# GpSimd computes the low part of the two weight units for the dilated heads' keys in place of VectorE

## What is computed

```python
for l in range(DEPTH):
    h = rms_norm(x, g_mix[l])
    proj = h @ w_in[l]
    ...
    qa = (rms_norm(c_q, q_norm[l]) @ w_uq[l]).reshape(b, s, HEADS_A, QK_NOPE + QK_ROPE)
    kva = (rms_norm(c_kv, kv_norm[l]) @ w_ukv[l]).reshape(b, s, HEADS_A, QK_NOPE + V_DIM_A)
    ...
    o_a = dense_attention(qa, ka, kva[..., QK_NOPE:])
    pb = p_b.reshape(b, s, 3, HEADS_B, HEAD_DIM)
    o_b = dilated_sliding_attention(rope(pb[:, :, 0], pos), rope(pb[:, :, 1], pos), pb[:, :, 2])
    ...
    x = x + mixed @ w_out[l]
    h2 = rms_norm(x, g_mlp[l])
    x = x + jnp.square(jax.nn.relu(h2 @ w_mlp_in[l])) @ w_mlp_out[l]
return rms_norm(x, g_final)
```

## Time and profile before

| | |
|---|---|
| median of 3 runs | 2924.04 us (2922.69 to 2928.27) |
| the profiled execution's own time | 2928.63 us |
| its span | 2926.6 us |
| TensorE busy | 2850.3 us (97%) |
| VectorE busy | 1719.2 us (59%) |
| ScalarE busy | 1057.6 us (36%) |
| GpSimd busy | 141.4 us (5%) |

### The profile page before, as it was taken

One profiled execution on the slowest core, in us unless ns is written; L12 is line 12 of the kernel. 1 busy time (PEld: TensorE's weight loads), 2 busy tenths in 40 slices (PEclk: granted clock), 3 DMA queues, 4 the chain that ended last, 5 costly groups with the idle time before them and its releaser, 6 DMA issues.

```text
span 2926.6 us, 39906 instructions
## 1 busy us (share of the span) xinstructions
PE 2850.3 (97%) x14640; PEld 2437.3 (83%) x14640; DVE 1719.2 (59%) x2998; ACT 1057.6 (36%) x1976; POOL 141.4 (5%) x253
## 2 busy tenths in 40 slices
PE   7999999999999999999998999999999999999998
PEld 7998788878888888888798988888788888888886
DVE  5651787885555455455666337788755455455457
ACT  5332777873311111111243236777732111111113
POOL 0000331000000000000000011300000000000000
PEclk9999999999999999999999999999999999999999
DMA  5556875313111111111146577743221111111111
GB/s 196 176 191 159 199 187 122 87 44 117 42 47 54 43 46 54 43 46 62 45 177 199 163 189 192 180 101 87 73 72 44 43 57 43 43 57 43 43 62 70
DMA packets 182359, 285.34 MB, mean 97 GB/s; under 512 B 48848, under 2 KB 138576, under 8 KB 172496
## 3 DMA queue, kind: packets, MB, share of 16 engines
q1 hardware_dynamic: 171600, 254.16, 29.9%
q0 software_dynamic: 10624, 29.41, 3.6%
HBM read 210.60 MB, written 72.88 MB: 97 GB/s over the span
## 4 chain that ended last, share of the span: by engine, by line
PE 85%; DVE 5%; issue 3%; DMA 3%; ACT 2%; DVEq 1%; SPq 0%; ACTq 0%; POOLq 0%
PE ps L1445 24%; PE ps L1265 20%; PE ps L1460 18%; PE ps L1340 7%; PE ps L1354 6%; PE ps L1386 5%; PE ps L1396 2%; PE ps L1231 1%; PE ps L1304 1%; DMA biasC<-in_bias_c 1%; DMA values<-vst 1%; PE ps L1379 1%; DVE x L1184 1%; DVE hn L925 1%; DVE vbuf L1171 1%
## 5 line engine op out<-in xcount | busy, mean ns | idle before, releaser
L1460 PE MATMUL ps<-w_dn,hid 128*128 128x512 f32 x3072 | 713.9, 391 | 1.3
L1445 PE MATMUL ps<-hT,w_up 128*128 128x512 f32 x3072 | 702.5, 389 | 3.3 <-DVE hT L908 3.3
L1460 PEld LDWEIGHTS ps<-w_dn,hid 128*128 128x128 f32 x3072 | 573.5, 188 | 132.9 <-DVE x L1184 14.0
L1445 PEld LDWEIGHTS ps<-hT,w_up 128*128 128x128 f32 x3072 | 576.1, 188 | 123.2 <-ACT rbuf L858 3.7
L1265 PE MATMUL ps<-ws,hT 128*128 128x384 f32 (+3 forms) x3072 | 608.6, 356 | 6.5 <-DVE hT L908 5.3
L1265 PEld LDWEIGHTS ps<-ws,hT 128*128 128x128 f32 x3072 | 536.0, 190 | 52.1 <-DVE hT L908 5.8
L1184 DVE TENSOR_TENSOR x<-ps,x 128x512 f32<-128x512 f32 x512 | 343.0, 688 | 224.2 <-PE ps L1460 224.0
L1171 DVE TENSOR_TENSOR vbuf<-rbuf 128x512 f32<-128x512 f32 x128 | 88.5, 692 | 371.0 <-ACT rbuf L858 371.0
L808 ACT ACTIVATE pT<-ps 128x512 fp32r<-128x512 f32 (+1 forms) x448 | 240.5, 582 | 144.0 <-PE ps L1354 141.9
L908 DVE TENSOR_TENSOR pT<-ps,pT 128x512 fp32r<-128x512 f32 (+1 forms) x448 | 281.4, 663 | 8.2 <-ACT pT L808 7.2
L858 ACT ACTIVATE rbuf<-ps 128x512 f32<-128x512 f32 x128 | 76.6, 598 | 553.9 <-PE ps L1445 553.9
(11 more groups left out here) (85 smaller groups left out, 2175.4 us busy)
## 6 DMA issues: line engine op xcount, KB each, us to landing
raw<-in_wstream SPq DMA_DIRECT2D x76, 1024.0 KB, 4.8
head<-feats SPq DMA_DIRECT2D x192, 256.0 KB, 6.3
feats<-tst SPq DMA_DIRECT2D x128, 192.0 KB, 2.5
values<-vst POOLq DMA_DIRECT2D x32, 384.0 KB, 3.1
head<-values SPq DMA_DIRECT2D x24, 512.0 KB, 4.0
biasC<-in_bias_c SPq DMA_DIRECT2D x16, 768.0 KB, 11.5
raw<-in_wstream SPq DMA_DIRECT2D x12, 768.0 KB, 5.9
x_park<-x SPq DMA_DIRECT2D x16, 512.0 KB, 8.9
```

Source lines behind the costliest of these rows:

```text
L1445: last = pe.matmul(ps[:, k % 2, :], w_up[slot_of(l, 1 if first else 0)][:, w1, kt, ft * P:(ft + 1) * P], hT[:, w2, kt, sh * 512:(sh + 1) * ...
L1460: last = pe.matmul(ps[:, 2 + m % 4, :], hid[slot_of(l + 1, slot)][:, w1, ft, s * P:(s + 1) * P], w_dn[slot_of(l, 0 if last_group else 1)][ ...
```

## The change

GpSimd computes the low part of units 6 and 7 of each layer, between its stores of values: unit 6 behind the store of `uv 1`, unit 7 behind that of `uv 2`. VectorE leaves both out, in both layers. Since `split_lo` is a plain counter which two engines now raise, GpSimd waits for the unit before, and VectorE, ahead of the `bv` units, for both `bk` units.

```diff
+            def split_rest(l, job, half):
+
+                u = unit_of(job, half)
+                n = unit_len(job, half)
+                off = half * unit_len(job, 0)
+                pool.wait_ge(split_hi, l * NU + u + 1)
+                pool.wait_ge(split_lo, l * NU + u + 2)
+                hold(pool)
+                s = ws[slot_of(l, SLOT[job])]
+                pool.tensor_tensor(s[:, LO, off:off + n], raw[:, u % 2, 0:n], words(s[:, HI, off:off + n]),
+                                   ALU.subtract).then_inc(split_lo, 1)
+
             for l in range(DEPTH):
                 for vt, e in enumerate(VSTAGED):
...
                                    words(vst[:, k, 0:nh, :].rearrange("p h d -> p (h d)"))).then_inc(vst_out[k], 16)
+                    if e[1:] in (("uv", 1), ("uv", 2)):
+                        split_rest(l, "bk", e[2] - 1)
...
                 dve.wait_ge(split_hi, l * NU + u + 1)
+                if job == "bv":
+                    dve.wait_ge(split_lo, l * NU + unit_of("bk", 1) + 1 + 2)
...
                     if e[0] == "split":
-                        split_job(l, e[1], e[2])
+                        if e[1] != "bk":
+                            split_job(l, e[1], e[2])
```

## The result

| | before | after |
|---|---|---|
| median of 16 runs each | 2924.41 us (2921.26 to 2928.27) | 2930.36 us (2925.07 to 2938.82) |
| ratio | | 1.0021, interval 1.0015 to 1.0028 |
| the profiled execution's own time | 2928.63 us | 2928.79 us |
| its span | 2926.6 us | 2927.0 us |

The change costs 6.0 us, 0.21%, with an interval of 0.15% to 0.28%. It lies inside the range that was forecast and just beyond the 0.2% named there. In both kernels TensorE has the same work in it.

The account below looks back on a forecast made before the run. TensorE, busy 97% of the span, was taken as the bound, with its next work hanging on R. Terms 7.2 - 0.55 + 2.9 = +9.6 us gave 2933.6 us on the median (2938.2 us profiled); range 2927 to 2943 us.

Parts of the forecast that it names:

- R: Moment ScalarE may write `ur 2` into `tst`, after stores of `bq 7`; forecast 7.2 us later in layer one, 0.55 earlier in two.
- the wait of its 13th matmul: In `acc bk 0`, TensorE would wait 1.6 and 1.3 us for GpSimd's unit 7, 2.9 us in all.
- the subtraction: One unit's low part on GpSimd, two passes over the inputs: 3.5 us, between 1.76 and 5.3 us.
- GpSimd's start on `uv 2`: GpSimd would store `uv 2` at R + 2.93, for 0.54 us, and then subtract unit 7.
- the reload: Ahead of GpSimd's first subtraction, in the first layer, an instruction listed as ISA would cost 6.0 us.
- the slow subtraction: Rival, chance 0.17: GpSimd's subtraction takes three passes, 5.3 us, and the reload 7.1 us; +17.9 us, 2942 us.
- reload for nothing: Rival, chance 0.14: the reload ahead of GpSimd's first subtraction costs nothing; R 1.2 us later in layer one, not 7.2.
- The landing behind the load: From SP's start of the load of unit 8 to R: 6.0 us, ends 5.5 and 7.7.
- the 2.72 us wait: TensorE's wait for VectorE's low parts near unit 6 would go or shrink, worth 0 while the ScalarE stall covers it.
- the waits for ScalarE: TensorE's stalls behind the wait for VectorE, 2.33 and 5.57 us before, would be about 10 and 5 to 8 us.
- VectorE held up by GpSimd: Rival, chance 0.12: VectorE's last `ur 2` instructions stand until GpSimd's subtraction ends; about +1 us on the forecast, 2934.6 us.
- what sets R is SP's order: SP starts unit 8's load before the stores of `bq 7`; R comes 7.7 and 9.4 us after the load's start.

Follow-up runs that it names:

- Unit 6 alone: The changed kernel with only unit 6's subtraction on GpSimd and unit 7 kept on VectorE: 2926.78 us, ratio 1.0012 to the kernel before.
- the pair of kernels with late loads: Kernel before and changed kernel, each with SP's loads of units 8 and 9 behind the stores of `ur 2` and `ur 3`: 2925.10 and 2933.37 us.
- The extra subtraction: Kernel before, plus a 1024-column GpSimd subtraction behind the stores of `uv 1` and `uv 2`, its result unused: 2924.12 us, ratio 0.9997.
- the best kernel: Kernel before with the load of unit 8 behind the stores of `ur 2` and VectorE's unit 6 behind the low part of `uq 2`: 2916.14 us, ratio 0.9971.

## Why the prediction was right, and where it was wrong

**Right: the direction and the two places. The size was partly luck.** The forecast was +9.6 us and slower; measured were +6.0 us, and the loss lies at the two places that it named, the chain from unit 6 to R and `acc bk 0` with the wait of its 13th matmul. Its sizes for the subtraction (3.5 us, measured 3.43 to 3.45), for SP's step behind it (0.08 us, measured 0.09), for GpSimd's start on `uv 2` (R + 2.93, measured R + 2.93 and R + 2.92) and for unit 7 (R + 7.12, measured R + 6.96 and R + 6.95) held. The 3.5 us were the author's estimate, two times 1.76 us; 3.44 us are 1.95 times the 1.76 us of the earlier trace rows. The 0.15 us for GpSimd's start was an allowance that no row gave; 0.10 and 0.01 us are measured. That TensorE would want unit 7 at R + 5.55 and R + 5.79 is an estimate too: of the 24 matmuls' 5.36 and 5.60 us the second twelve get 2.22 us, half of the 4.45 us of the next 24, and the first twelve the rest. The largest term of the sum, though, was not there at all, and only because other terms came out larger does the time lie just beyond the 0.2% and not at the +3.5 us of the forecast's own sum without it.

**The step that failed: the reload at 6.0 us.** It was 6.0 of the 9.6 us. No run shows this term, nor the 7.1 us that the slow subtraction has in its place. The first subtraction of the program starts 0.10 us behind the store, with the two rows of 37 ns in front of it, and that of the second layer, which has no such rows, 0.01 us behind its own. So the instruction costs at most 0.1 us where it could delay anything; "reload for nothing", which makes R 1.2 us later in the first layer and not 7.2, was the true case. What the instruction does, and whether some of its work lies where GpSimd stood idle, no run here shows.

**The rest was mis-sized the other way.** Without the reload the forecast's own sum was 1.2 - 0.55 + 2.9 = +3.5 us; the stretch shows +5.4. The landing behind the load was good: 6.0 us assumed, 5.78 and 6.81 measured, and R moved by +0.85 and +0.06 where +1.2 and -0.55 were forecast without the reload. The second layer's `acc bk 0` went as forecast, with a slow first half and a wait of 1.26 us: 9.36 us from R to its end, where the forecast's terms make 9.31. The first layer's took 10.92 us where they make 9.38. The forecast had the first half slow there too, as before, and the second at 2.2 us. But TensorE's wait for ScalarE was short now (0.51 us), the transposes and the first twelve matmuls ran at a clock of 1.00 (0.60 and 2.33 us), and TensorE was at the 13th at R + 4.18 and waited 2.83 us in place of 1.6. That longer wait is no loss of its own, since unit 7 came when it was forecast. The loss is what followed: the second twelve took 3.91 us, at a mean clock of 0.56, in place of 2.2. That the clock can be low behind the wait was in no term of the sum.

**Wrong: the 2.72 us wait was to shrink, and the waits for ScalarE were to be about 10 and 5 to 8 us.** The first grew to 4.62 and 4.54 us, and the others fell to 0.51 and 1.90. (There are two such waits in each layer, not three as the prediction says.) The forecast was right that the wait for VectorE is worth 0 as long as ScalarE's stall covers it, and this cut both ways: the growth cost little or nothing either. Unit 6 alone shows the exchange (4.62 up, 0.24 left), and the pair of kernels with late loads shows the price of the whole change where the cover is gone, 8.3 us.

**The rival that came true beside it: VectorE held up by GpSimd.** It was given 0.12 and +1 us. The hold is there at all four subtractions, 3.73 to 3.82 us each, and it is why VectorE's busy time rose: 4 x (3.76 - 0.25) = +14.0, less 4 x 1.76 = 7.0, makes +7.0 of the 7.8 us. VectorE's addition is recorded 0.16 to 0.27 us ahead of GpSimd's subtraction each time, and is held all the same. The price was right in kind: the stores of `bq 7` started 1.00 us behind the load (119.64 to 120.64) where 0.35 were assumed. The extra subtraction shows that a shorter hold, covered, costs nothing that can be measured; but no run here had the delay of the units without a hold, so what each has of the 6.0 us stays open.

**Right in the main: R hangs on SP's order.** With the load moved behind the stores, R comes some 3 us earlier in each layer; the forecast's "what sets R is SP's order" was too strong, since 3.30 and 4.90 us of waiting for the stores remain. What this place had to give was in the order, of SP's load and of the subtraction among VectorE's own instructions, not in VectorE's busy time.

## What to carry to other kernels

Before work is moved off an engine because others wait for it, ask what they wait for next: here the wait for VectorE stood in front of a longer chain (a buffer behind stores, the stores behind a load), and changing the order of one load and one subtraction gave 8.2 us where moving the subtraction to an idle engine lost 6.0. An idle GpSimd is not a free one: here it took twice as long for the same subtraction (3.44 against 1.76 us), an addition of VectorE with both inputs in SBUF stood until it had ended (3.73 to 3.82 us in place of 0.25), and whoever needed the result waited for the slower engine (TensorE 2.83 and 1.26 us at the 13th matmul). A covered stall hides a loss as well as a gain, so that each edit's price depends on whether the cover is still there.

## What the runs showed of the hardware

- GpSimd's subtraction of 128 x 1536 numbers took 3.43 to 3.45 us in the changed kernel, where VectorE took 1.76 us for the same one in the kernel before.
- VectorE stayed held across three GpSimd subtractions issued one behind the other (4.10 us for one addition of 96 columns that takes 0.25 us like its neighbour). Four of its operations with one input in PSUM were not held: beside the extra subtraction (116.05 to 118.91) L965 and L966 kept their 0.25 us.
- GpSimd was held too: in the kernel with the extra subtraction it took 2.86 us for 1024 columns where 0.66 us of them lay beside VectorE's subtraction, and 3.63 us where 1.39 us did. There VectorE's subtraction had started first. In the changed kernel VectorE's addition is recorded first as well, by 0.16 to 0.27 us, and is the one that is held; what decides is not settled by these rows.
- GpSimd's memsets held another kind of operation: beside them (117.31 to 119.15) a VectorE copy of 32 columns from SBUF to SBUF took 0.95 us in place of 0.17 and ended with them, while VectorE's additions with both inputs in SBUF kept 0.26 and 0.25 us (117.90 and 118.07).
- TensorE's granted clock in `acc bk 0` of the changed kernel was 1.00 behind waits of 0.51 and 1.26 us and 0.51 behind one of 2.83 us; twelve matmuls of 384 columns took 2.33 and 2.35 against 3.91 us. The length of the wait alone doesn't tell. In the second layer a wait of 1.90 us, behind 18 matmuls that had run at a mean clock of 0.59 (4.78 us, against 3.01 us at 1.00 before), was followed by six transposes at 1.00 (0.60 us) and then by twelve matmuls at 0.55 (3.90 us). In the best kernel the same twelve took 2.33 us at 1.00 behind a wait of 2.11 us, with matmuls at 1.00 ahead of it (1554.00:1556.78).
- An increment that GpSimd issues by itself behind memsets came at their start, not at their end, in both layers (load at 117.43, memsets from 117.31 to 119.15; load at 1557.60, memsets from 1557.48 to 1559.32).
